# Four edits to an encoder kernel: GpSimd's order in the scan, VectorE's order beside the convolution taps, the place of the key sums, and the input norm's root

## The chip, the cores and the metric

The kernel runs on one core of a Trainium2 chip, in one launch. The metric is the device time of one execution in microseconds, the median of several. The engines of the core are TensorE (PE, matmuls and transposes; PEld are its weight loads), VectorE (DVE), ScalarE (ACT), GpSimd (POOL) and SyncE (SP), which here does nothing but issue transfers and wait. Each engine runs its own instructions in order; semaphores join them.

## The reference

A hybrid encoder layer is applied to two groups of tokens, 512 and 1024 of them, with model width 1024, in float32:

```
h = rms_norm(x);  p = h @ w_in                       # 4832 columns
z = centred_shift(p[RWKV columns]);  u = p[conv columns];  gates = sigmoid(rest)
A = rwkv7(z)      # 8 heads of 64, forward and reverse scans summed, group norm, bonus
B = silu(layer_norm(depthwise_conv31(glu(u))))
x = x + (gate_a * A @ W_o_rwkv + gate_b * B @ W_o_conv) @ w_out
x = x + expert_choice_ffn(rms_norm(x))               # 16 experts, each takes its top tokens
y = rms_norm(x)
```

with `rms_norm(x) = x * rsqrt(mean(x*x) + 1e-6) * g`. In the RWKV branch each direction has `decay = exp(-exp(logw))`, the keys are normalised per head (`kk / max(norm(kk), 1e-12)`), and per token and head the state follows `S = S diag(decay) + (S a) b^T + v k^T`, `y = S r`, with `a = -kk` and `b = kk * rate`.

## The kernel before

The kernel has five phases, one after the other: `project`, `scan`, `mixing`, `experts`, `final_norm`. The change touches the first two.

**project.** The 1536 tokens are three blocks of 512. The input is normalised first: ScalarE squares x, TensorE sums the squares into a PSUM bank with a matrix of ones, ScalarE takes the root (`root`, L618), VectorE the reciprocal (L811) and then scales x by it (L802); ScalarE splits the result into a high part, VectorE and GpSimd take the low part. Then 38 tiles of 128 columns are projected. Each product is made of three matmuls (high x high, low x high, high x low), for eight slices k of the contraction and three blocks: 72 matmuls of 128x512 per tile. From tile 2 on, small units of TensorE's work are put between the slices of a tile, at the places that `small_units` gives as (tile, k). They share two PSUM banks in turn, so unit u waits until unit u - 2 has been read (`emptied`).

The tiles stand in the order `ORDER`: two low-rank tiles, then four groups of eight (key, value, receptance, conv gate, conv input, three merge gates), then the remaining merge gates. Engines other than TensorE go through steps s = 1 to 38; step s treats tile s - 1 while TensorE works on tile s. Each group has six pieces (three blocks in two directions), one per step, from the group's fourth step on. For a piece p:

- TensorE makes two "rate" products at k = 1 and 2; ScalarE turns them into f0 and f1 by a sigmoid (`rates`, L695), after it has copied the next tile's weights (`high`, L607).
- VectorE scans f0 into f2 (`decay_sum`, L889), GpSimd takes the difference (L571), ScalarE three exponentials (L701, L703, L705), GpSimd writes AR (L579, L584).
- VectorE does `factors` (L898 to L910): it needs f1 and the first exponential f3 and writes KB.
- In the next step TensorE transposes both in three units "turn" at k = 4, 5, 6, ScalarE copies them out (L729), SyncE stores them.

Between `decay_sum` and `factors` VectorE has its share of the convolution: 31 taps per group, three to six in a step (`taps_at`, L846; the last, tap 30, is L850 and writes `conv`, which SyncE stores). In the step after the second tile of a group the keys are normalised: three "keys" units (L498), `key_max` (L876), logarithm and exponential on ScalarE (L744, L748), `key_normalise` (L882), and three "values" transposes.

SyncE's order in one step is: the load of the next weight tile (L347); the store of the first turned copy; a wait for GpSimd's last product and the store of AR (L404); the other stores of the last piece (L361, L369); a wait for VectorE's KB and its store (L414); in the step of tap 30 a wait for it and the conv store (L419).

**scan.** The recurrence is done in 24 chunks of 64 tokens, both directions side by side. Chunk i has a chain step `body(i)` on TensorE, which starts with `level_n(d, i, 0)` (L1175) and needs X0, the chunk's inverted 16x16 blocks placed on a diagonal. These are prepared ahead: masked products of chunk i + 4 are made in chain step i, stored (`lower`) and loaded again as 16x16 blocks of a pair of chunks (`diagonal`, gb); GpSimd inverts the pair (`invert`, L1399 to L1406: one addition, 14 rounds of two small instructions, a copy); SyncE stores the result (`inverses`, L1096) and loads it per chunk (`compact`, L1107, xc); GpSimd places it (`expand`, L1414, once for each direction). `expand` waits for xc and for the chain step two back. GpSimd's loop has, for even i, the inversion of pair i/2 + 1 and then the placement for chunk i + 1; for odd i the placement alone.

Of the kernel before, what the change touches and what calls it, by code (L numbers as in the profile page):

```python
# [9 lines left out]
ACT = mybir.ActivationFunctionType  # L10
# [4 lines left out]
D = 1024  # L15
# [190 lines left out]
def small_units():  # L206

    units = {}
    for s in range(N_TILES):
        p, last = piece_at(s), piece_at(s - 1)  # L210
        if p is not None:
            units[s, 1], units[s, 2] = ("rate", p, 0), ("rate", p, 1)
        if last is not None:
            for n in range(3):
                units[s, 4 + n] = ("turn", last, n)
            if last % 2 == 1:
                units[s, 7] = ("bonus", last // 2, 0)
        if s - 2 in GROUP_AT:
            hp = GROUP_AT.index(s - 2)
            for b in range(NB):  # L220
                units[s, b], units[s, 4 + b] = ("keys", hp, b), ("values", hp, b)
    return units


# [11 lines left out]
def project(nc, a, g):  # L236


    with ExitStack() as ctx:
        sb = lambda name, shape, dt=F32: ctx.enter_context(nc.sbuf_tensor(name, shape, dt))  # L240
        sem = nc.alloc_semaphore
# [35 lines left out]
        square = [halves(2 * (NB if b != 1 else 2)) for b in range(NB)]  # L277

        x_in = [[sem(f"p_x_in{b}{h}") for h in range(2)] for b in range(NB)]
        squared, halved, summed, rooted, normed = (  # L280
            sem(f"p_{n}") for n in ("squared", "halved", "summed", "rooted", "normed"))
        up_split, dup_in, rank_high, rank_low = (sem(f"p_{n}") for n in ("up_split", "dup_in", "rank_high", "rank_low"))
        h_high_done, h_low_v, h_low_p = sem("p_h_high_done"), sem("p_h_low_v"), sem("p_h_low_p")
        up_in, w_in, w_high_done, w_split = sem("p_up_in"), sem("p_w_in"), sem("p_w_high_done"), sem("p_w_split")
# [56 lines left out]
        with nc.Block() as block:  # L341
# [260 lines left out]
            def _(act):  # L602
# [12 lines left out]
                def root(b):  # L615
                    act.wait_ge(summed, 2 * b + 2)
                    act.wait_ge(normed, KD * b)
                    nc.scalar.activation(inv, g.bank[6 + b % 2][:], ACT.Sqrt, bias=g.c("eps", 0, 1),  # L618
                                         scale=1.0 / D).then_inc(rooted, 1)

                def h_top(b):
                    for n in range(4):
# [161 lines left out]
            def _(dve):  # L784
# [23 lines left out]
                ch.link(ts(mu_own[:], mu_own[:], -1.0, 1.0, ALU.mult, ALU.add))  # L808
                for b in range(NB):
                    dve.wait_ge(rooted, b + 1)  # L810
                    ch.link(nc.vector.reciprocal(inv, inv))  # L811
                    if b == 1:
                        fold(2)
                    scale(b, range(0, 4))
                    low(b, 0)
                    scale(b, range(4, KD))
                    low(b, 3)
# [74 lines left out]
                def factors(p):  # L892
                    hp, b, d = piece(p)
                    dve.wait_ge(a_rate, 2 * p + 2)
                    own_k = f4 if d else k_first
                    if d:
                        dve.wait_ge(m_bonus, p // 2)
                    ch.link(ts(own_k, f1, -1.0, g.v("k_a", hp), ALU.add, ALU.mult))  # L898
                    ch.count(stt(own_k, own_k, 1.0, key[:, tok(b)], ALU.add, ALU.mult))
                    dve.wait_ge(v_nkk, NB * (hp + 1))  # L900
                    ch.link(stt(f1, f1, -1.0, nkk[:, tok(b)], ALU.mult, ALU.mult))
                    dve.wait_ge(a_exp, 3 * p + 1)
                    dve.wait_ge(kb_out, 16 * p)
                    dve.wait_ge(m_turn, 3 * p)
                    tt(KB[:, :, 0, :], four(own_k), four(f3), ALU.mult).then_inc(v_k, 1)
                    tt(KB[:, :, 1, :], four(f1), four(f3), ALU.mult).then_inc(v_b, 1)
                    dve.wait_ge(v_k, p + 1)
                    if d:
                        ch.link(tt(f4, f4, k_first, ALU.add))
                        stt(f4, f4, g.v("r_k", hp), val[:, tok(b)], ALU.mult, ALU.mult).then_inc(v_w, 1)  # L910

                for s in range(1, N_TILES + 1):
                    t, tile = s - 1, ORDER[s - 1]
                    if tile < N_CONV and tile % 2 == 0:
                        convolve_in(t, tile // 2)
                    elif tile >= T_LORA:
                        shift(t, tile)
                    if s == 3:
                        rank_rest()
                    if s - 1 in GROUP_AT:  # L920
                        key_scale(GROUP_AT.index(s - 1))
                    if s - 2 in GROUP_AT:
                        key_max(GROUP_AT.index(s - 2))
                    p, taps = piece_at(s), taps_at(s)
                    if p is not None:
                        decay_sum(p)
                    for i, tap in taps:
                        convolve(i, tap)
                    if s - 2 in GROUP_AT:
                        key_normalise(GROUP_AT.index(s - 2))  # L930
                    if p is not None:
                        factors(p)


BASE = 16
# [4 lines left out]
def scan(nc, a, g):  # L940


    DIRS = range(2)
# [4 lines left out]
    with ExitStack() as ctx:  # L948
# [78 lines left out]
        with nc.Block() as block:  # L1027
# [358 lines left out]
            def _(pool):  # L1386
# [35 lines left out]
                for d in DIRS:  # L1422
                    expand(d, 1)
                for i in range(1, NCH - 1):
                    if i % 2 == 0 and i + 2 < NCH:
                        invert((i + 2) // 2)
                    for d in DIRS:
                        expand(d, i + 1)

            @block.vector  # L1430
            def _(dve):
# [1408 lines left out]
```

## Time and profile before

| | |
|---|---|
| median of 3 runs | 2781.54 us (2779.42 to 2785.18) |
| the profiled execution | 2781.26 us |
| its span, first to last instruction | 2779.5 us |
| TensorE busy | 2469.4 us (89%) |
| VectorE busy | 1842.3 us (66%) |
| ScalarE busy | 1200.2 us (43%) |
| GpSimd busy | 745.6 us (27%) |

`project` runs to about 837 us of the span, `scan` from there to about 1310 us. Times in the rows below are counted from the start of the span. In a row of the timeline the number in brackets is how long the engine sat idle before the instruction, with what ended that; "x4" means four like instructions merged into one row, and the duration is then from the first start to the last end. SPq and ACTq are transfers being issued; the duration is that of the issue, not of the transfer. The granted clock is 1.00 where TensorE runs at its full 2.4 GHz and 0.50 where it runs at 1.2 GHz. Names like `work` are one large buffer with many parts.

### The profile page before, as it was taken

Reading aid. Unit: us, or ns where it says so; the run is one execution under the profiler, and the core shown is the slowest. Engines: PE = TensorE matmul, PEld = TensorE weight load, DVE = VectorE, ACT = ScalarE, POOL = GpSimd, SP = SyncE. Lnnn points to the kernel's source line nnn. Section 1 sums busy time; section 2 is a strip of 40 time slices with the busy share of each in tenths; the row PEclk is TensorE's granted clock in tenths of the full one; section 3 lists DMA queues with packets and bytes.
Section 4 is the critical chain, followed back from the end, with each engine's and each line's share of the span. In section 5 each row is a group of like instructions: output and inputs, shape, how many; then the busy total and the mean of one; then the engine's idle time right before and its main releaser. Section 6 shows DMA issues by size and latency. Waiting matters only on the chain. (4 is left out here: it accounts for less than half of the span.)

```text
span 2779.5 us, 50229 instructions
## 1 busy us (share of the span) xinstructions
PE 2469.4 (89%) x19612; PEld 2083.9 (75%) x19612; DVE 1842.3 (66%) x2471; ACT 1200.2 (43%) x1746; POOL 745.6 (27%) x689
## 2 busy tenths in 40 slices
PE   6999989999895799897499899499999999999992
PEld 4777767777675788887267676399889998899991
DVE  7448868678674455554585857577777777777773
ACT  4443444334421233332233431365555656555552
POOL 3134342443420334332444533200101110001100
PEclk9999999999996899999699999699999999999996
DMA  3234243342435566652454543677777777777745
GB/s 129 73 106 129 72 138 98 117 130 80 134 127 160 153 173 178 170 141 77 150 191 164 192 155 114 256 231 247 239 255 237 228 247 241 245 247 229 246 162 200
DMA packets 294149, 476.87 MB, mean 172 GB/s; under 512 B 142048, under 2 KB 209776, under 8 KB 266336
## 3 DMA queue, kind: packets, MB, share of 16 engines
q1 hardware_dynamic: 280048, 428.25, 47.3%
q0 software_dynamic: 7680, 26.82, 4.7%
q10 hardware_dynamic: 6256, 19.47, 2.0%
q8 instruction: 120, 1.97, 0.3%
q14 instruction: 45, 0.37, 0.0%
HBM read 362.20 MB, written 110.69 MB: 170 GB/s over the span
## 5 line engine op out<-in xcount | busy, mean ns | idle before, releaser
L2499 PE MATMUL bank<-e_xt,e_w_high 128*128 128x384 f32 x1792 | 525.4, 357 | 1.3 <-DVE e_xt L2635 1.3
L2622 DVE TENSOR_TENSOR e_w_low<-e_w,e_w_high 128x2048 fp32r<-128x2048 f32 x192 | 436.2, 2286 | 95.8 <-ACT e_w_high L2555 95.8
L2500 PE MATMUL bank<-e_xt,e_w_low 128*128 128x192 f32 x1792 | 449.4, 251 | 0.0
L2555 ACT ACTIVATE e_w_high<-e_w 128x2048 fp32r<-128x2048 f32 x192 | 366.1, 1908 | 108.5 <-PE bank L2521 82.3
L2500 PEld LDWEIGHTS bank<-e_xt,e_w_low 128*128 128x128 f32 x1792 | 342.6, 191 | 0.6
L2499 PEld LDWEIGHTS bank<-e_xt,e_w_high 128*128 128x128 f32 x1792 | 338.4, 189 | 2.7 <-issue 1.4
L846 DVE SCALAR_TENSOR_TENSOR work<-work,vec 128x1551 f32<-128x1551 f32 x116 | 278.6, 2402 | 3.2
L463 PE MATMUL bank<-h_high,w_high 128*128 128x512 f32 x864 | 267.9, 419 | 0.3 <-DVE work L863 0.3
L466 PE MATMUL bank<-h_low,w_high 128*128 128x512 f32 x864 | 250.0, 398 | 0.0
L469 PE MATMUL bank<-h_high,w_low 128*128 128x512 f32 x864 | 247.5, 395 | 0.0
L2445 POOL DMA_INDIRECT xacc_dram<-e_y,e_put x32 | 50.3, 1573 | 731.6 <-DVE e_y L2657 726.8
L560 POOL TENSOR_TENSOR w_low<-w,w_high 128x1024 fp32r<-128x1024 f32 x38 | 94.0, 2475 | 436.7 <-ACT w_high L607 436.7
L466 PEld LDWEIGHTS bank<-h_low,w_high 128*128 128x128 f32 x864 | 165.9, 192 | 37.2
L469 PEld LDWEIGHTS bank<-h_high,w_low 128*128 128x128 f32 x864 | 165.6, 192 | 36.7
L463 PEld LDWEIGHTS bank<-h_high,w_high 128*128 128x128 f32 x864 | 154.3, 192 | 46.7 <-issue 24.0
L2666 DVE TENSOR_TENSOR e_sums<-bank,e_sums 128x192 f32<-128x192 f32 x256 | 79.3, 351 | 140.6 <-ACT e_sums L2580 140.6
L1748 POOL TENSOR_TENSOR x_w_low<-x_w,x_w_high 128x1024 fp32r<-128x1024 f32 x48 | 119.4, 2488 | 178.3 <-ACT x_w_high L1994 178.2
L889 DVE TENSOR_TENSOR_SCAN work<-con,work 128x512 f32<-128x512 f32 x24 | 57.0, 2375 | 152.2 <-issue 88.4
L2580 ACT ACTIVATE e_sums<-bank 128x192 f32<-128x192 f32 x256 | 70.6, 328 | 153.6 <-PE bank L2503 153.5
L607 ACT ACTIVATE w_high<-w 128x1024 fp32r<-128x1024 f32 x38 | 40.2, 1057 | 212.9 <-DMA w<-in_w_in 212.9
L1325 ACT ACTIVATE xx<-bank 128x512 f32<-128x512 f32 (+1 forms) x96 | 47.1, 491 | 158.7 <-PE bank L1188 97.4
L2459 PE MATMUL bank<-e_w_high,e_hid_parts 128*128 128x512 f32 x256 | 104.7, 409 | 0.0
(313 smaller groups left out, 5313.2 us busy)
## 6 DMA issues: line engine op xcount, KB each, us to landing
e_w<-in_ew SPq DMA_DIRECT2D x192, 1024.0 KB, 5.5
features_dram<-work SPq DMA_DIRECT2D x48, 512.0 KB, 3.2
fe<-features_dram SPq DMA_DIRECT2D x24, 1024.0 KB, 6.5
x_w<-in_w_mix SPq DMA_DIRECT2D x48, 512.0 KB, 3.8
w<-in_w_in SPq DMA_DIRECT2D x38, 512.0 KB, 4.6
ba_tok_dram<-work SPq DMA_DIRECT2D x96, 128.0 KB, 2.3
gates_dram<-work ACTq DMA_DIRECT2D x16, 768.0 KB, 4.1
all<-ba_tok_dram SPq DMA_DIRECT2D x96, 128.0 KB, 3.1
```

The costliest lines, as they stand in the source:

```text
L463: nc.tensor.matmul(bank(t, b)[:], w_high[t % 2][:, c], h_high[:, k, tok(b)], start=(k == 0), stop=False)
L466: nc.tensor.matmul(bank(t, b)[:], w_high[t % 2][:, c], h_low[:, k, tok(b)], start=False, stop=False)
L469: mm = nc.tensor.matmul(bank(t, b)[:], w_low[t % 2][:, c], h_high[:, k, tok(b)], start=False, stop=(k == KD - 1))
L560: tt(w_low[t % 2][:], w[:], w_high[t % 2][:].bitcast(F32), ALU.subtract).then_inc(w_split, 1)
L846: ch.link(stt(acc, cin[:, tap:tap + n_acc], wt, acc, ALU.mult, ALU.add))
L1748: tt(w_low[s % 2][:], w[s % 2][:], w_high[s % 2][:].bitcast(F32), ALU.subtract).then_inc(w_split, 1)
L2459: nc.tensor.matmul(out, left[0], right[0], start=first, stop=False)
L2499: nc.tensor.matmul(*wide, start=(k == 0), stop=False)
L2500: nc.tensor.matmul(*narrow, start=False, stop=False)
L2555: nc.scalar.activation(w_high[n % RING][:], w[n % RING][:], ACT.Copy).then_inc(w_high_done, 1)
L2622: tt(w_low[n % RING][:], w[n % RING][:], w_high[n % RING][:].bitcast(F32), ALU.subtract)\
L2666: ins = tt(half, g.bank[4 + 2 * (f % 2) + side][:, 0:SLOTS], half, ALU.add)
```

## The change

1. `small_units`: the key units of a group's second tile go from k = 0, 1, 2 to k = 1, 2, 4, the value units from 4, 5, 6 to 5, 6, 7.
2. `root`: instead of a square root on ScalarE and a reciprocal on VectorE, ScalarE takes the logarithm of the mean square and the exponential of minus one half of it.
3. VectorE in `project`: of a step's taps only the first stays ahead of `key_normalise` and `factors`; the others follow them.
4. GpSimd in `scan`: in an even step the placement for chunk i + 1 comes first, the inversion second.

```diff
-                units[s, b], units[s, 4 + b] = ("keys", hp, b), ("values", hp, b)
+                units[s, (1, 2, 4)[b]], units[s, 5 + b] = ("keys", hp, b), ("values", hp, b)
...
-                    nc.scalar.activation(inv, g.bank[6 + b % 2][:], ACT.Sqrt, bias=g.c("eps", 0, 1),
-                                         scale=1.0 / D).then_inc(rooted, 1)
+                    nc.scalar.activation(inv, g.bank[6 + b % 2][:], ACT.Ln, bias=g.c("eps", 0, 1),
+                                         scale=1.0 / D).then_inc(logged, 1)
+                    act.wait_ge(logged, b + 1)
+                    nc.scalar.activation(inv, inv, ACT.Exp, scale=-0.5).then_inc(rooted, 1)
...
-                    ch.link(nc.vector.reciprocal(inv, inv))
...
-                    for i, tap in taps:
+                    for i, tap in taps[:1]:
                         convolve(i, tap)
                     if s - 2 in GROUP_AT:
                         key_normalise(GROUP_AT.index(s - 2))
                     if p is not None:
                         factors(p)
+                    for i, tap in taps[1:]:
+                        convolve(i, tap)
...
                 for i in range(1, NCH - 1):
+                    for d in DIRS:
+                        expand(d, i + 1)
                     if i % 2 == 0 and i + 2 < NCH:
                         invert((i + 2) // 2)
-                    for d in DIRS:
-                        expand(d, i + 1)
```

## Rows read from the trace of the kernel before

**Rows 1.** Waits of TensorE, 100 to 830 us: total, times, longest in us.

```profile
PE bank L493 <- ACT work L695: 30.9, 12, 4.8
PE bank L498 <- DVE work L876: 6.5, 3, 2.7
```

**Rows 2.** The same view, 912 to 1310 us.

```profile
PE bank L1175 <- POOL x L1414: 38.3, 15, 10.2
```

**Rows 3.** Timeline of GpSimd in `scan`: start, duration, then the instruction.

```profile
1010.11 0.73 POOL L1399 TENSOR_TENSOR xb<-gb,masks 128x256 f32<-128x256 f32 x1 [10.50 <-DMA gb<-g_dram]
...
1021.46 2.04 POOL L1414 TENSOR_TENSOR x<-xc,masks 128x512 f32<-128x512 f32 x2
1034.30 2.04 POOL L1414 TENSOR_TENSOR x<-xc,masks 128x512 f32<-128x512 f32 x2 [10.80 <-DMA xc<-x_dram]
```

**Rows 4.** Timeline of SyncE, the same stretch.

```profile
1008.22 0.99 SPq L1107 DMA_DIRECT2D xc<-x_dram  x2
...
1027.04 0.49 SPq L1096 DMA_DIRECT2D x_dram<-xb  x1
...
1031.62 1.10 SPq L1107 DMA_DIRECT2D xc<-x_dram  x2
```

**Rows 5.** Timeline of TensorE, starts of two odd chain steps.

```profile
952.94 1.37 PE L1175 MATMUL bank<-x,nl 64*64 64x64 f32 x18 [10.19 <-POOL x L1414]
...
1022.55 0.68 PE L1175 MATMUL bank<-x,nl 64*64 64x64 f32 x16 [2.80 <-POOL x L1414]
```

**Rows 6.** Windows of odd chain steps: length, busy per engine, clock, DMA share, GB/s.

```profile
1022.50:1039.40 16.90, 16.53 (x384) 15.78 (x384) 8.85 (x17) 5.41 (x11) 3.03 (x3) 0.90 0.51 127
1056.60:1072.10 15.50, 15.18 (x386) 14.40 (x386) 8.92 (x17) 5.41 (x11) 3.47 (x3) 1.00 0.51 128
...
1123.10:1140.80 17.70, 17.70 (x384) 17.04 (x384) 8.84 (x17) 5.41 (x11) 2.95 (x3) 0.84 0.41 107
1159.70:1176.30 16.60, 16.55 (x384) 15.84 (x384) 8.88 (x17) 5.41 (x11) 3.03 (x3) 0.90 0.45 110
```

**Rows 7.** Timeline of GpSimd, another even placement.

```profile
1172.34 2.04 POOL L1414 TENSOR_TENSOR x<-xc,masks 128x512 f32<-128x512 f32 x2 [11.64 <-DMA xc<-x_dram]
```

**Rows 8.** Windows of two tiles with key sums.

```profile
277.30:302.30 25.00, 22.45 (x92) 16.99 (x92) 20.97 (x18) 12.15 (x17) 2.81 (x1) 0.93 0.20 57
...
113.30:133.70 20.40, 20.40 (x92) 15.83 (x90) 7.76 (x10) 11.36 (x16) 2.39 (x1) 1.00 0.11 31
```

**Rows 9.** Timelines of VectorE and SyncE in one step of `project`.

```profile
404.11 10.31 DVE L846 SCALAR_TENSOR_TENSOR work<-work,vec 128x1551 f32<-128x1551 f32 x4
...
412.82 0.36 SPq L404 DMA_DIRECT2D features_dram<-work  x1
...
415.53 1.25 SPq L369 DMA_DIRECT2D k_tok_dram<-work  x1
417.63 0.39 SPq L414 DMA_DIRECT2D features_dram<-work  x1
```

**Rows 10.** Waits of SyncE, 100 to 830 us.

```profile
SPq L414 <- DVE work L906: 40.1, 22, 4.4
```

**Rows 11.** Timelines of VectorE and SyncE in a step with tap 30.

```profile
340.57 3.01 DVE L850 SCALAR_TENSOR_TENSOR work<-work,vec 128x512 f32<-128x512 f32 x2
...
346.80 0.36 SPq L414 DMA_DIRECT2D features_dram<-work  x1
```

**Rows 12.** Timelines of ScalarE and VectorE in the input norm.

```profile
16.84 1.28 ACT L618 ACT_TABLE_LOAD   x1
...
54.08 0.67 ACT L618 ACTIVATE work<-bank,con 128x512 f32<-128x512 f32 x1
...
55.41 3.34 DVE L811 RECIPROCAL work<-work 128x512 f32<-128x512 f32 x1
```

**Rows 13.** Timeline of ScalarE behind the logarithm of the keys.

```profile
465.12 1.28 ACT L748 ACT_TABLE_LOAD   x1
466.42 1.68 ACT L748 ACTIVATE work<-work 128x512 f32<-128x512 f32 x3
```

More of the change, by code:

```diff
@@ L279, in project @@
         x_in = [[sem(f"p_x_in{b}{h}") for h in range(2)] for b in range(NB)]
-        squared, halved, summed, rooted, normed = (
-            sem(f"p_{n}") for n in ("squared", "halved", "summed", "rooted", "normed"))
+        squared, halved, summed, logged, rooted, normed = (
+            sem(f"p_{n}") for n in ("squared", "halved", "summed", "logged", "rooted", "normed"))
         up_split, dup_in, rank_high, rank_low = (sem(f"p_{n}") for n in ("up_split", "dup_in", "rank_high", "rank_low"))
```

## Prediction

> **What bounds the kernel.** The change touches the first two phases, `project` and `scan`, so I read them alone: first the waits of TensorE, then the engines behind each wait in order of time, then windows for the clock. In both phases TensorE is the pacemaker, and its waits are few and named. In `project` [rows 1] it waits 30.9 us, 12 times, for ScalarE's sigmoids at L695 (in front of a transpose, because the PSUM bank has to be free) and 6.5 us, three times, for VectorE's L876 (in front of the third key sum). In `scan` [rows 2] it waits 38.3 us for GpSimd's L1414, which places the inverted 16x16 blocks. Each class belongs to one of the edits. A reader should see next whether the awaited instruction is late through its own inputs or through its place in a queue, and what stands behind it when it is moved.
>
> **Edit 1, blocks ahead of the inversion (scan).** In every even step GpSimd inverts a pair of chunks and only then places the blocks of the next, odd chunk. [Rows 3]: the inversion starts at 1010.11, the two placements at 1021.46, so it takes 11.35 us, and TensorE starts that chain at 1022.55 after 2.80 us of idleness [rows 5]. The blocks were requested at 1008.22 and 1.0 later [rows 4]; a request of this kind lands 2.7 us after its issue (1031.62 in [rows 4], placement at 1034.30 in [rows 3]), so they lie there at about 1011.9, ten microseconds before they are used. Placed first, they are done at 1011.9 + 2.04 = 1013.9, and the wait goes; the largest, 10.19 us at 952.94 [rows 5], goes likewise. All 38.3 us hang on this one order.
>
> The stall also costs clock. The chain step after a short stall takes 15.5 us at granted clock 1.00 (full, the 2.4 GHz level); after stalls of 2.8 us and more they take 16.6 and 16.9 us at 0.90, 17.7 us at 0.84, so part of them ran at the 1.2 GHz level [rows 6]. Six steps follow such a stall and are as slow (the rows, 1.1 to 2.2 us too long, stand for them); six at 1.5 us give 9 us, and the step after the first stall I leave aside.
>
> What is moved back: the inversion starts at 1013.9 instead of 1010.11 and ends at 1025.2. Its result leaves only at 1027.04, since SyncE is still issuing other transfers [rows 4], so nothing is late by that; the blocks of the next even chunk are placed at 1034.30 to 1036.34 as before, and its chain started at 1039.4 [rows 3, 6], with 3.1 us to spare. The pair of steps, however, gets shorter by 2.8 + 1.4 = 4.2 us, so a wait of about 1 us appears there. Elsewhere the even blocks are placed later in the pair: 1172.34 to 1174.38 [rows 7], for a chain that starts at 1176.3 [rows 6], 1.9 us of slack against a saving of some 5: 3 us are late next. Over ten pairs, most with more slack than this last one, I take 5 us back (bounds 0 and 12). Sum: 38.3 + 9 - 5 = 42 us. Bounds: 38.3 - 12 = 26 (no clock back, all pairs tight) and 38.3 + 12 = 50.
>
> **Edit 2, key sums later (project).** The tile with the first key sums, at 113.3, has no wait and takes 20.4 us; the next of its kind takes 25.0 us at clock 0.93 [rows 8], because the third sum needs a bank that VectorE has not read yet. Moved from places 0, 1, 2 to 1, 2, 4, the third comes two products later (a place is some 2 us: the 20.4 us of the tile less the units' 4, over eight) plus the shifts, about 4 us, more than the longest wait (2.7 [rows 1]). This tile gives 4.6 us; the two others have the remaining 3.8 us of the 6.5 [rows 1] and little clock to regain, about 4.5: 9 us. The value transposes move one place back, so SyncE's last store of values and the weight load behind it, and with them the next sigmoids, are about 2 us later; they have room, as no transpose waits for a sigmoid in the next tile. Bounds: 5 (a remnant wait in each) and 10.
>
> **Edit 3, factors ahead of most taps (project).** The sigmoids wait for ScalarE's copy of the next weights, which waits for their transfer, which SyncE issues behind the store of KB, which waits for VectorE's factors; and these stood behind four taps, 10.31 us [rows 9]. It looks like 7.7 us per piece (three taps). But SyncE first waits for GpSimd's last factor and then issues the stores of the previous piece: 412.82 the AR store, 415.53 the k store, taking 1.25, and KB at 417.63 [rows 9]. KB could go at 416.8: 0.85 us earlier, not 7.7. GpSimd's chain (scan, difference, exponential, two products) does not depend on the taps. SyncE's 22 waits for KB sum to 40.1 us, at most 4.4 [rows 10], and the longest stand in the first step of a group, where the next transpose has time to spare. So three of the six pieces of a group give 0.3 to 2.2 us each, some 3 us per group, carried along from one late step to the next.
> In the step with tap 30 it is different: SyncE also waits there for the last tap, since the conv store stands between KB and the weight load. Now the last tap, L850, ends at 343.58, the factors follow, and KB goes at 346.80 [rows 11]: factors 3.2 us. Behind them come the two instructions of the bonus, about 1.4 at 0.7 each. In the new order these 4.6 us lie ahead of L850, which would end at 343.58 + 4.6 = 348.2. Its scan starts some 3 us sooner (the first step's long KB wait is gone), but the factors then wait 1 to 2 us for their exponential: about 346.4. Then conv store and load go, 0.4 us sooner than today, and KB's issue of 0.4 is already past: 0.8 gained. The longest waits of the phase, 4.8 us [rows 1], stand in the tiles after these steps, and stay, with the clock they cost.
> Sum: four groups of about 2.5 us with their share of clock: 8 us (I take off some, as the weight load then competes with stores issued just before it). Bounds: 0 (the landing does not move) and 16 (all gaps with their clock). VectorE's work in a step is 10.3 of taps, 3.2 to 4.6 of factors and some 3 of scan, 16.5 to 18 us where a tile takes 20 and more, so the taps are not late; its new wait for the exponential of the same piece costs 1 to 2 us of that idleness, with only taps queued behind it.
>
> **Edit 4, ln and exp for the root.** VectorE's reciprocal takes 3.34 us, ScalarE's root before it 0.67 [rows 12]. Instead ScalarE loads a table, 1.28, takes ln, loads again, 1.28 [rows 13], and takes exp; ln and exp I price as the root, for the same shape: 1.28 + 0.67 + 1.28 + 0.67 = 3.9 us against 0.67 + 3.34 = 4.0. Block 0: the first load stands there already [rows 12], so 1.28 + 0.67 replace 3.34: 1.4 us earlier. Block 1: nothing of its own, but it starts earlier by that gain, less a little for the later load of x. Block 2: from 54.08 the new chain ends at 58.0; the reciprocal, begun at 55.41, ended at 58.75: 0.7 more. TensorE waits for the normalised input in each block: 1.7 us. Bounds: -1 (the third x block, whose load now goes 2 us later, is late) and 2.5.
> The trace has ln and exp with a load each, and the first activation starts 0.02 us after a load [rows 13]. The Trainium skill ("ScalarE: Activation LUTs", sections "What ACT_TABLE_LOAD costs" and "Table sets: the hidden batching unit") says otherwise on both: a switch costs 1.28 us plus a drain of 1.38, and one set holds ln and exp. By its drain the new chain would be 2.8 us longer, and this edit would cost about 1 us instead of giving 1.7; by the shared set it would give 1.3 us more per block. The trace shows neither, and I go by it.
>
> **Sum.** 42 + 9 + 8 + 1.7 = 61 us. The profiled execution took 2781.26 us (its span 2779.5), 0.3 from the median of 2781.54, so 2781.3 - 61 = 2720 us. What comes after `scan` waits for its end and moves as a whole; the taps that run out after the last piece end with the same distance to TensorE's end as now.
>
> **Rivals.**
> A. *The freed time is taken back by the even chains* (SyncE and the transfers set the pace of a pair of steps): for it speaks that the even placements wait for the transfer of their blocks (10.80 and 11.64 us [rows 3, 7]) with 2 to 3 us to spare; against it, that GpSimd's inversion is not what SyncE waits for. Then only the slack and the first stall come: 10.19 and the slack, 9 x 1.9 = 17, so 27 with no clock, and with a tap gain of 2 the sum is 27 + 9 + 2 + 1.7 = 40: 2741.
> B. *The factors remove all the sigmoid waits*: the 30.9 us [rows 1] and, at 1.5 us for each of some ten tiles, 15 us of clock: 46 instead of 8. Time 2720 - 38 = 2682. For it speaks the chain as written in the code; against it [rows 9, 11].
> C. *Slower: the inversion slips behind the blocks.* If the odd blocks land L us after the inversion's input, the inversion ends L + 2.04 + 11.35 after it; its result leaves 16.9 after it now (1027.04 - 1010.11 [rows 3, 4]), and the even chain has 3.1 to spare. So from L = 6.6 each even chain is late by the rest, and the whole kernel is slower when ten pairs lose more than edits 2 to 4 give: 10 x (L - 6.6) > 19, L above 8.5. With L = 10, and the odd chains no better off than now: 2781 + 34 - 19 = 2796. Against it: L is 1.8 here.
> D. *The new order does nothing*, since the placement of the odd blocks waits for TensorE as well (two chains back): 2781 - 19 = 2762. Against it: where a placement waited, it waited for the transfer [rows 3, 7].
>
> **How the numbers follow.** Forecast 0.62 (2705 to 2735), A 0.22, B 0.07, D 0.04, C 0.05. The lower bounds of all edits together give 26 + 5 + 0 - 1 = 30 us, the upper ones 50 + 10 + 16 + 2.5 = 78: the range 2700 to 2750 takes these and A in and leaves B, C and D out. A change under 0.2% (5.6 us) can't be told from none here. Faster 0.94, same 0.02, slower 0.04.
>
> **What would show it.** In the profile after: TensorE's wait for L1414 (x) all but gone in odd steps and small in even ones, chain steps of 15 to 15.5 us at clock 1.00, `scan` about 42 us shorter; GpSimd's placements in pairs right before each inversion. In `project`: no wait in front of the key sums; the sigmoid wait still 4 to 5 us in the tile after tap 30, three times, and 1 to 4 in the two tiles of a group that had it. TensorE's first product at about 26.3 instead of 27.7. I am wrong if even chains wait over 1 us each in the mean (A), or if the sigmoid waits sum to under 10 us (B).

## The result, and the profile after

The changed kernel takes 2710.25 us in the median of 4 runs (2705.57 to 2715.02), the kernel before beside it 2780.48: a ratio of 0.9755, 95% interval 0.9716 to 0.9795. The forecast was 2720, range 2700 to 2750. The profiled execution of after took 2707.34 us, its span 2705.6, which is 73.9 less than before. By stages of the span: up to tile 2 it is 1.6 us shorter, tiles 2 to 37 34.3 us, from there to the first chain step 3.0, chain steps 0 to 23 36.8, and the rest is 1.9 longer.

Two windows carry most of it; the columns are as in [rows 6]. First before, tiles 2 to 37 and chain steps 0 to 23, then the same work after:

```profile
80.60:814.10 733.50, 695.93 (x3073) 542.77 (x3074) 520.50 (x383) 304.13 (x381) 263.25 (x131) 0.97 0.37 111
892.73:1293.53 400.80, 350.79 (x8416) 333.97 (x8416) 214.48 (x390) 130.16 (x259) 149.33 (x376) 0.92 0.58 156
```

```profile
78.90:778.10 699.20, 681.83 (x3072) 534.33 (x3073) 505.50 (x382) 301.70 (x380) 220.74 (x131) 0.99 0.39 117
853.76:1217.77 364.01, 340.36 (x8416) 323.98 (x8417) 212.27 (x390) 130.08 (x259) 151.88 (x376) 0.96 0.64 171
```

The same matmuls keep TensorE busy 14.1 and 10.4 us less, at a higher granted clock; the rest of the 34.3 and 36.8 us is idleness that went. In `project` something else shrank that no edit touches in number or shape: GpSimd's busy time, from 263 to 221 us over the same 131 instructions.

TensorE's waits after, in `project` (answers to [rows 1]; the wait for the key maxima is gone) and in `scan` (to [rows 2]; this window also holds 6.2 us in front of chain step 1, which lies ahead of the window of [rows 2] and was 5.8 there):

```profile
PE bank L493 <- ACT work L697: 17.3, 9, 3.7
```

```profile
PE bank L1178 <- POOL x L1417: 12.6, 5, 6.2
```

GpSimd in one pair of chain steps (answers to [rows 3]): the placement of the odd blocks stands right in front of the inversion, whose first instruction is L1402 and whose last is L1409; the even placement still waits for its transfer. (The profile names L1195 of TensorE as what ended the first wait; why it was a transfer there too is said under rival D.)

```profile
957.88 2.04 POOL L1417 TENSOR_TENSOR x<-xc,masks 128x512 f32<-128x512 f32 x2 [7.96 <-PE bank L1195]
959.88 0.73 POOL L1402 TENSOR_TENSOR xb<-gb,masks 128x256 f32<-128x256 f32 x1
...
970.63 1.05 POOL L1409 COPY xb<-xb 128x256 f32<-128x256 f32 x1
978.68 2.04 POOL L1417 TENSOR_TENSOR x<-xc,masks 128x512 f32<-128x512 f32 x2 [7.00 <-DMA xc<-x_dram]
```

Windows of chain steps 7, 8 and 13 (answers to [rows 6]) and of the tile with the second key sums (to [rows 8]):

```profile
271.00:291.40 20.40, 20.40 (x92) 15.84 (x92) 15.38 (x16) 11.33 (x16) 2.39 (x1) 1.00 0.14 44
968.98:983.93 14.95, 14.95 (x388) 14.30 (x385) 9.50 (x18) 6.00 (x12) 4.29 (x9) 1.00 0.56 139
983.93:1000.23 16.30, 15.22 (x388) 14.43 (x384) 10.05 (x19) 6.00 (x12) 9.03 (x24) 1.00 0.85 246
1060.22:1079.30 19.08, 16.70 (x389) 15.92 (x385) 9.72 (x19) 6.00 (x12) 7.21 (x19) 0.91 0.62 168
```

A step without idleness takes 14.95 us; nine of the 23 do, of either parity. The two longest take 19.1 and 19.2 us (13 and 17): TensorE stops inside each, the first time for 2.38 us, with nothing that the profile shows to wait for. The largest wait for a placement is in front of chain step 22. TensorE, two starts:

```profile
1065.72 0.37 PE L1195 MATMUL bank<-x,t 64*64 64x64 f32 x1 [2.38 <-issue]
```

```profile
1203.09 1.69 PE L1178 MATMUL bank<-x,nl 64*64 64x64 f32 x24 [3.84 <-POOL x L1417]
```

### The profile page after: what moved, and what is told of

The parts are those of the page before. It is cut to its first block and busy times, and to the rows that moved or that the text cites. A ratio compares the mean times of both kernels' runs of the same rounds, so it can differ in the third digit from the quotient of the medians.

```text
span 2705.6 us, 50239 instructions
## 1 busy us (share of the span) xinstructions
PE 2443.5 (90%) x19612; PEld 2062.2 (76%) x19612; DVE 1817.4 (67%) x2468; ACT 1205.4 (45%) x1753; POOL 704.2 (26%) x689
## 5 line engine op out<-in xcount | busy, mean ns | idle before, releaser
L2558 ACT ACTIVATE e_w_high<-e_w 128x2048 fp32r<-128x2048 f32 x192 | 365.9, 1908 | 108.6 <-PE bank L2524 82.4
L847 DVE SCALAR_TENSOR_TENSOR work<-work,vec 128x1551 f32<-128x1551 f32 x116 | 216.1, 1863 | 2.4
L560 POOL TENSOR_TENSOR w_low<-w,w_high 128x1024 fp32r<-128x1024 f32 x38 | 91.0, 2396 | 441.3 <-ACT w_high L607 441.3
L1417 POOL TENSOR_TENSOR x<-xc,masks 128x512 f32<-128x512 f32 x48 | 49.4, 1046 | 250.3 <-DMA xc<-x_dram 242.4
```

Of the source, the lines that this page charges most:

```text
L560: tt(w_low[t % 2][:], w[:], w_high[t % 2][:].bitcast(F32), ALU.subtract).then_inc(w_split, 1)
L847: ch.link(stt(acc, cin[:, tap:tap + n_acc], wt, acc, ALU.mult, ALU.add))
L2558: nc.scalar.activation(w_high[n % RING][:], w[n % RING][:], ACT.Copy).then_inc(w_high_done, 1)
```

## The experiments

Ten kernels ran, each timed beside the kernel before. In short (ratios with their 95% interval; "to chain 0" is where the first chain step starts in the span, 892.7 before and 853.8 after):

| kernel | edit | median, us | ratio | to chain 0 |
|---|---|---|---|---|
| e1_blocks | edit 1 alone | 2735.29 | 0.985 (0.9809 to 0.9892) | 886.4 |
| e2_taps | edit 3 alone | 2748.32 | 0.9901 (0.9872 to 0.993) | 858.5 |
| e3_keys | edit 2 alone | 2776.73 | 1.0007 (0.9985 to 1.0028) | 889.6 |
| e4_root | edit 4 alone | 2773.63 | 0.9991 (0.9974 to 1.0009) | 887.7 |
| e5_kb_late | before; weight load ahead of KB's store | 2752.69 | 0.9915 (0.9886 to 0.9945) | 858.7 |
| e8_ends_last | e5; copy of the ends behind the product | 2744.78 | 0.9887 (0.9856 to 0.9918) | 858.3 |
| e9_ends_act | e5; that copy on ScalarE | 2746.63 | 0.9899 (0.9883 to 0.9916) | 857.8 |
| e10_no_tap_ahead | after; no tap ahead of the factors | 2706.33 | 0.9754 (0.9738 to 0.977) | 851.6 |
| e6_load_early_old | before; weight load ahead of all waits | 2724.23 | 0.9803 (0.9772 to 0.9834) | 835.1 |
| e7_load_early_new | after; the same | 2680.47 | 0.9661 (0.9634 to 0.9689) | 828.3 |

The kernel before measured 2776.34 us beside e1 to e4, 2775.41 beside e5 to e8 and 2774.88 beside e9 and e10. The last column is from one profile each: e1, whose `project` is that of before, has 886.4 where before has 892.7, so differences of up to some 6 us say nothing there.

Where the time of tiles 2 to 37 goes is seen best by kinds of tile (sums in us, from the starts of the tiles in one profile each). The rows are the tiles behind tap 30 (15, 23, 31), two sets that also wait for sigmoids (9, 17, 25, 33 and 10, 18, 26, 34), the tiles whose key sums waited (12, 20, 28), and the rest. e4, which changes nothing in these tiles, shows how much one profile says: up to 7 us in a row, mostly moved from one row to the next, and 3 in the sum.

| tiles | before | e4 | e2 | e3 | e5 | after | e10 | e6 | e7 |
|---|---|---|---|---|---|---|---|---|---|
| 15, 23, 31 | 81.6 | 82.7 | 77.9 | 87.3 | 66.0 | 77.1 | 82.9 | 60.9 | 60.9 |
| 9, 17, 25, 33 | 100.8 | 94.0 | 82.4 | 97.4 | 94.3 | 83.1 | 81.5 | 81.2 | 81.2 |
| 10, 18, 26, 34 | 86.0 | 91.2 | 85.1 | 87.3 | 82.2 | 84.6 | 80.4 | 78.5 | 78.5 |
| 12, 20, 28 | 70.6 | 67.8 | 64.6 | 61.2 | 64.6 | 61.2 | 61.2 | 62.3 | 61.2 |
| the rest | 394.5 | 395.2 | 392.9 | 397.2 | 393.5 | 393.2 | 393.2 | 392.9 | 393.2 |
| all | 733.5 | 730.8 | 702.8 | 730.4 | 700.5 | 699.2 | 699.2 | 675.9 | 675.0 |

### The four edits alone

```diff
# e1_blocks
                 for i in range(1, NCH - 1):
+                    for d in DIRS:
+                        expand(d, i + 1)
                     if i % 2 == 0 and i + 2 < NCH:
                         invert((i + 2) // 2)
-                    for d in DIRS:
-                        expand(d, i + 1)
# e2_taps
-                    for i, tap in taps:
+                    for i, tap in taps[:1]:
                         convolve(i, tap)
...
+                    for i, tap in taps[1:]:
+                        convolve(i, tap)
# e3_keys
-                units[s, b], units[s, 4 + b] = ("keys", hp, b), ("values", hp, b)
+                units[s, (1, 2, 4)[b]], units[s, 5 + b] = ("keys", hp, b), ("values", hp, b)
# e4_root: the logarithm and exponential of the change, no reciprocal
```

> The kernel before with edit 1 alone (GpSimd places the blocks ahead of the inversion). The forecast's theory: TensorE's waits for the placement (38.3 us) leave all odd chain steps and the clock comes back; scan from the first to the last chain step, 400.8 us before, comes to about 363 as in the changed kernel, project stays as it was, time about 2742 (-38). Rival (the parts need each other, since the phases share nothing but their border): another figure than the changed kernel's scan. Rival A (even chains take it back): over 370 us.

> The kernel before with edit 3 alone (factors ahead of most taps). Theory of the forecast (only the wait for KB goes): 8 us less, GpSimd's instructions as long as before (product L579 1.98 us, copy L582 1.63 us). New theory from the two traces (VectorE's taps beside GpSimd's work slowed it, and GpSimd's last product releases the stores and the weight load): L579 1.43 us, L582 0.50 us in the mean, TensorE's waits for the sigmoids 31 to about 17 us, project 25 us shorter, time about 2755.

> The kernel before with edit 2 alone (key sums at places 1, 2, 4). Theory: the 6.5 us of waits in front of the third key sum go, the three tiles take 20.4 us each, 9.3 us less: 2771. Rival: without the other edits VectorE is later, so that part of the wait stays: 3 to 6 us less.

> The kernel before with edit 4 alone (ln and exp for the inverse root). Theory: TensorE's first tile behind the three blocks starts 1.7 us earlier (78.9 instead of 80.6), nothing else changes: 2779. By the drain of 1.38 us that the Trainium skill names beside each table load (ScalarE: Activation LUTs, What ACT_TABLE_LOAD costs) it would start about 1 us later than before.

Against the 2776.34 beside them: -41.1, -28.0, +0.4 and -2.7 us, together -71.4, where all four at once gave -70.2. So the edits add up, but not as forecast (42, 8, 9, 1.7).

e1: TensorE's wait for the placements, 870 to 1310 us, a window that again holds chain step 1 (6.1 us; the 6.4 is in front of chain step 22):

```profile
PE bank L1175 <- POOL x L1414: 15.7, 6, 6.4
```

Chain steps 0 to 23 take 362.9 us (400.8 before). The four profiles with the new order (e1, e7, e10 and after) have 362.9 to 364.5 us here, the others with the old one 394.0 to 405.3, so the order is the cause. The even chains take back 9.6 us of waiting in e1, 6.4 in the changed kernel.

e3: the key tiles take 20.4 us, as forecast, and the sigmoids take it away again. TensorE's waits in `project`:

```profile
PE bank L493 <- ACT work L695: 40.1, 13, 6.8
```

Against [rows 1] the wait for L695 rises from 30.9 to 40.1 us; the tiles behind tap 30 go from 27.2, 27.8 and 26.6 us to 28.7, 28.8 and 29.8. The reason is VectorE. Between 255 and 350 us it waited before for L677, 5.2 us, and has no such pause in e3, first row before, second e3:

```profile
DVE work L859 <- ACT work L677: 5.2, 2, 4.9
```

```profile
DVE work L859 <- ACT work L677: 0.3, 1, 0.3
```

TensorE's 4.6 us in the key tile bring tap 30 only 3.0 us forward (its start goes from 340.6 to 337.6), because VectorE is the one that is full up to there. Tiles 2 to 37 are 3.1 us shorter in all, no more than in e4, and the time is the same. The rival comes nearer than the theory, but even its 3 to 6 us are not there.

e4: the 1.7 us can't be read off the span. Tile 2 starts at 79.3 in e4 (forecast 78.9, before 80.6), but at 78.4 in e1, which has the old root: this start shifts between profiles by more than the edit gives. Under edit 4 below, the gain is counted from the second square instead.

e2: with the taps moved alone, both waits fall, and so does the key wait, whose tiles and units this kernel leaves where they were (6.5 to 2.2 us). Edit 3 alone makes the three key tiles 6.0 us shorter, of the 9.3 in the changed kernel. Its waits:

```profile
PE bank L493 <- ACT work L695: 16.8, 8, 3.5
...
PE bank L498 <- DVE work L876: 2.2, 3, 1.0
```

### Which link of the loop: e5, e8, e9, e10

From one piece to the next there is a loop: scan, GpSimd's chain, store of AR, other stores, (KB), issue of the weight load, its landing, weights copied, sigmoids, next scan. In the step of [rows 9] it takes 11.5 + 5.3 + 5.6 + 1.7 = 24.2 us (scan to the store of AR, that to the issue of the load, landing, to the next scan), where a tile without a stall takes 19.5 to 20.3. After the change the same step has 9.8 + 5.0 + 6.1 + 1.7 = 22.6.

```diff
# e5_kb_late (before, SyncE's order)
+                ahead = [s for s in range(1, N_TILES - 2) if piece_at(s) is not None and (not taps_at(s) or taps_at(s)[-1][1] < TAPS - 1)]
...
-                    if s + 1 < N_TILES:
+                    if s + 1 < N_TILES and s - 1 not in ahead:
                         load(s + 1)
...
+                    if s in ahead:
+                        load(s + 2)
                     if p is not None:
                         sp.wait_ge(v_b, p + 1)
# e8_ends_last (e5; SyncE's wait, GpSimd's chain)
-                        sp.wait_ge(l_r, p + 1)
+                        sp.wait_ge(l_ar, p + 1)
...
-                    nc.gpsimd.tensor_copy(g.ends[:, d, hp, 8 * b:8 * b + 8], ...)
-                    tt(AR[:, :, 1, :], four(val[:, tok(b)]), four(f2), ALU.mult).then_inc(l_r, 1)
+                    tt(AR[:, :, 1, :], four(val[:, tok(b)]), four(f2), ALU.mult).then_inc(l_ar, 1)
+                    nc.gpsimd.tensor_copy(g.ends[:, d, hp, 8 * b:8 * b + 8], ...).then_inc(l_r, 1)
# e9_ends_act (e5): that copy is an activation on ScalarE
# e10_no_tap_ahead (after)
-                    for i, tap in taps[:1]:
+                    for i, tap in taps[:0]:
...
-                    for i, tap in taps[1:]:
+                    for i, tap in taps[0:]:
```

> The kernel before, taps in their old order; SyncE issues the next weight load ahead of the store of KB (not in the steps with tap 30). So the load no longer waits for VectorE's factors, while the taps still run beside GpSimd's work. Theory (two causes: the KB wait some 8 us, the slowed GpSimd instructions the rest of the 30): 8 to 12 us less in project, L579 and L582 as long as before (1.98 and 1.63 us). Rival (the KB wait was all, and my 8 us were mis-summed): as much as edit 3 alone gave, 28 us.

e5 brings the first chain step to 858.7, as e2 does (858.5), with the taps where they were: the loop of the same step is 11.6 + 2.7 + 6.6 + 1.7 = 22.5 us. In time it is -22.7 us where e2 is -28.0, with intervals that overlap: the theory's 8 to 12 us were far too few, the rival's 28 is nearer. In e2 nothing waits for KB either and GpSimd's chain is 1.7 us shorter besides, but KB's issue stays ahead of the load, and the loop of that step is 9.8 + 5.0 + 6.1 + 1.7 = 22.6 us, the same.

That the two sums are alike is chance, though, for the table above has them in different tiles. e5 takes 15.6 of its 33.0 us out of the tiles behind tap 30: in the first step of a group (13, 21, 29) the load now follows the store of AR by 0.4 us instead of 5.2. e2 gains 3.7 us there, since its factors now lie ahead of tap 30, for which SyncE waits, and 18.4 of its 30.8 us in tiles 9, 17, 25 and 33, where e5 gains no more than e4 differs by (6.5 and 6.8). The two loops ahead of tile 17 are 3.6 us shorter in e2, 3.3 of it in GpSimd's chain (9.3 to 7.6 and 11.5 to 9.9 us). So the wait for KB and GpSimd's chain are two causes, and each shows in tiles of its own.

The chain on GpSimd, 100 to 790 us (the columns: busy time, mean ns of one, idle time before them): before, then after.

```profile
L571 POOL TENSOR_TENSOR work<-work 128x512 f32<-128x512 f32 x24 | 61.1, 2545 | 27.9 <-DVE work L889 27.9
L579 POOL TENSOR_TENSOR work<-work 128x512 f32<-128x512 f32 x24 | 47.5, 1981 | 25.0 <-ACT work L703 25.0
L582 POOL COPY ends<-work 128x8 f32<-128x8 f32 x24 | 39.1, 1628 | 0.0
```

```profile
L571 POOL TENSOR_TENSOR work<-work 128x512 f32<-128x512 f32 x24 | 61.3, 2555 | 27.9 <-DVE work L890 27.9
L579 POOL TENSOR_TENSOR work<-work 128x512 f32<-128x512 f32 x24 | 34.4, 1433 | 28.9 <-ACT work L705 28.9
...
L582 POOL COPY ends<-work 128x8 f32<-128x8 f32 x24 | 12.0, 501 | 0.0
```

A copy of 128x8 takes 1.63 us before and 0.50 after; of 128x512, before, three instructions of one shape take 2.5, 2.0 and (L584, in both kernels) 1.3. The taps, beside which they stand, change as well: before, then after.

```profile
L846 DVE SCALAR_TENSOR_TENSOR work<-work,vec 128x1551 f32<-128x1551 f32 x102 | 248.9, 2440 | 2.7
```

```profile
L847 DVE SCALAR_TENSOR_TENSOR work<-work,vec 128x1551 f32<-128x1551 f32 x116 | 216.1, 1863 | 2.4
```

e8 and e9 ask how: if the copy is slow by itself, moving it away frees its time.

> As e5_kb_late, and GpSimd's copy of the ends (L582, 1.63 us) goes behind its last product, which alone releases the store of AR. Theory: GpSimd's chain sets the load of the weights, so the 1.6 us come off each late step: 10 to 16 us beyond e5_kb_late. Rival (SyncE's issues and the landing set it): nothing beyond e5_kb_late.

> The kernel before, with the next weights' load issued ahead of the store of KB in every step but those of tap 30 (as in e5), and GpSimd's copy of the chunk ends (1.4 us a piece there) given to ScalarE, behind its exponentials of the next piece. Theory 1 (GpSimd's chain of a piece, through the AR store on SyncE, sets when the load is issued): scan to AR store falls from 11.5 to about 10 us, `project` gets 5 to 15 us shorter than in e5, 2738 to 2748 us. Rival (what is slowed beside the taps is whatever GpSimd instruction stands there, as in e8, so the chain loses little): scan to AR store at 11 or more and a time within 5 us of e5's 2752.7. A second rival: the copy on ScalarE pushes its sigmoids or copies of weights back, and it is slower than e5.

Neither does: scan to AR store stays at 11.4 us in both (11.5 in e5), and the times are 7.9 and 6.1 us under e5's median (each against its own "before": ratios 0.9887 and 0.9899 beside 0.9915, intervals that overlap). Tiles 2 to 37 take 700.2 and 698.9 us where e5 has 700.5. That e9's time lies in its theory's 2738 to 2748 is luck: the chain did not get shorter. The product that moved into the copy's place takes 2.5 us instead of 1.3. First e8, then e9:

```profile
L585 POOL TENSOR_TENSOR work<-work 128x512 f32<-128x512 f32 x24 | 60.0, 2499 | 0.0
...
L586 POOL COPY ends<-work 128x8 f32<-128x8 f32 x24 | 31.2, 1301 | 0.0
```

```profile
L584 POOL TENSOR_TENSOR work<-work 128x512 f32<-128x512 f32 x24 | 60.4, 2518 | 0.0
```

The timelines say why. In the step of [rows 9] GpSimd's chain is this, and the second of the four taps is the row behind it:

```profile
404.26 2.80 POOL L571 TENSOR_TENSOR work<-work 128x512 f32<-128x512 f32 x1 [1.16 <-DVE work L889]
407.81 2.04 POOL L579 TENSOR_TENSOR work<-work 128x512 f32<-128x512 f32 x1 [0.74 <-ACT work L703]
409.80 1.74 POOL L582 COPY ends<-work 128x8 f32<-128x8 f32 x1
411.50 1.29 POOL L584 TENSOR_TENSOR work<-work 128x512 f32<-128x512 f32 x1
```

```profile
405.95 2.75 DVE L846 SCALAR_TENSOR_TENSOR work<-work,vec 128x1551 f32<-128x1551 f32 x1
```

The first tap runs alone from 404.11 [rows 9] to 405.9, 1.8 us; L571 was issued at 404.26, ends at 407.06, and that is 405.9 and nearly a whole L571 of 1.29 us. The second tap is issued at 405.95 and ends at 408.70, 1.8 us behind 406.9. L579 ends 1.15 us behind that, the third tap 1.8 us behind about 409.7; the copy ends with the third tap, at 411.54; L584 starts before the fourth tap and takes its 1.29. So the two engines take turns, one whole instruction each: each start and end fits that to about 0.2 us. In e9 the last product is issued at 395.71 into the third tap (394.63 to 397.39) and ends at 398.54:

```profile
395.71 2.83 POOL L584 TENSOR_TENSOR work<-work 128x512 f32<-128x512 f32 x1
```

```profile
394.63 2.75 DVE L851 SCALAR_TENSOR_TENSOR work<-work,vec 128x1551 f32<-128x1551 f32 x1
```

Dropping the copy only let the product run into that tap. What helps is a short instruction of VectorE at that place. After the change factors of 0.69 us stand there, and now they are the ones that wait (0.69 to 1.8 us):

```profile
392.35 1.79 DVE L902 SCALAR_TENSOR_TENSOR work<-work 128x512 f32<-128x512 f32 x1
394.18 1.81 DVE L906 TENSOR_TENSOR work<-work 128x512 f32<-128x512 f32 x1
```

The Trainium skill ("SBUF — State Buffer", section "Who interferes with whom") has this as a rule: VectorE and GpSimd share a port pair, and it is an exclusive lock; a VectorE instruction with two SBUF inputs contends with a GpSimd instruction that reads SBUF. That whoever issues first gets the pair "for the whole instruction" it says of VectorE's two-port modes. The trace agrees, and has whole turns for these two-input instructions as well, in numbers above. It was the rule that spoke against the forecast's size for edit 3, and the prediction did not weigh it.

> The changed kernel with no tap at all ahead of the factors (one was left there). Theory 1 (a tap beside GpSimd's difference L571 slows it to 2.55 us): L571 falls towards 2.0, scan to AR store from 9.8 to about 9.2 us, and the time is 3 to 10 us under the changed kernel's 2710. Rival: the first tap only filled VectorE's wait for the exponential of the same piece; VectorE then stands idle, its taps end later, the conv store behind tap 30 and the load behind it are later by one tap's 1.9 us in the three tap-30 steps, and the time is the same or up to 6 us longer.

The first tap, too, is such a holder: without it L571 falls from 2.56 to 1.45 us, and scan to AR store from 9.8 to 9.05 us in the plain steps. But the time is unchanged, a ratio of 0.9754 against 0.9755. TensorE's waits in `project` there:

```profile
PE bank L493 <- ACT work L697: 16.9, 5, 5.4
```

Five instead of nine, but the three tiles behind tap 30 wait 5.3 to 5.4 us each instead of 3.5 to 3.7: tap 30 is later. By the table, what is lost behind tap 30 (5.8 us) is won in the two rows below it. Both theories had a half of it.

### The load taken out of the loop: e6 and e7

```diff
+                ahead = [s for s in range(1, N_TILES - 2) if piece_at(s) is not None]
...
                     if last is not None:
                         staged(("turn", last, 0))
+                    if s in ahead:
+                        load(s + 2)
                     if p is not None:
                         hp, b, d = piece(p)
                         sp.wait_ge(l_r, p + 1)
```

> The kernel before, taps in their old order; in steps with a piece SyncE issues the next weight load right behind the first turned copy's store, ahead of its waits for GpSimd and VectorE. Theory (the weight load is the only way by which taps and factors reach TensorE): all sigmoid waits go, also those behind tap 30; project 45 us shorter, about 2732. Rival (ScalarE's sigmoid needs f1, that is VectorE's factors, in time): waits of 1 to 3 us stay in the steps with four taps.

> The changed kernel with the same early weight load. Theory: the 17.3 us of sigmoid waits and their clock, 25 us, leave project: about 2686, the fastest of all; its project is equal to that of e6_load_early_old but for the key sums (9 us), since the order of the taps then no longer matters. Rival (transfers compete: the load meets the stores of gates and turned copies): 10 us only.

In both TensorE waits for no sigmoid and no key maximum at all between 90 and 740 us, and the first chain step starts 51 to 58 us earlier in e6 and 58 to 64 in e7, by which of the two profiles of the old `project` one takes. So the load is the only way by which taps, factors and GpSimd's chain reach TensorE, and the rival of e6 falls; the granted clock is 1.00 over tiles 2 to 37 in both. In time e6 is -51.2 us, and e7, which has edit 1 as well, -94.9. e7 is the fastest kernel of the study: 2680.47 us, 24.7 us further below the kernel before beside it than the changed kernel is (-94.9 against -70.2), 29.8 by the bare medians. Its tiles 2 to 37 take 675.0 us where e6 has 675.9. With the load early neither the order of the taps nor the place of the key sums is worth anything there: the 9 us expected for the key sums are 1.1 in the three key tiles. Its SyncE in the same step: the load goes ahead of the store of AR, and its landing takes 3.8 us.

```profile
381.22 0.50 SPq L347 DMA_DIRECT2D w<-in_w_in  x1
385.19 0.36 SPq L407 DMA_DIRECT2D features_dram<-work  x1
```

## Why the prediction came out as it did

The sign and the time were right, and the mechanism of edit 1, which is the larger part. Of edits 2 and 3 the forecast had the waits right and the sizes wrong, one too large and one far too small; that their errors partly cancel is luck.

**Edit 1 (42): right.** -41.1 us alone. In the profiles chain steps 0 to 23 are 36.8 us shorter, 37.9 in e1. The waits fell from 38.3 to 6.4 (12.6 less the 6.2 of chain step 1), TensorE is busy 10.4 us less (the clock, forecast 9), and the even chains take 6.4 us of waiting (forecast 5). Its places were less good: chain step 8, for which 1 us was forecast, has none, chain step 16 0.8 instead of 3; the largest, 3.8, is at 22. The stops inside steps 13 and 17, 2.4 us each, were not foreseen.

**Edit 2 (9): too large.** In the changed kernel the three key tiles are 4.6, 1.6 and 3.1 us shorter, 9.3 in all, but 6.0 of that is there with edit 3 alone (e2), so beside edit 3 the edit is worth some 3 us; alone it gives nothing (e3). The step that failed is "they have room, as no transpose waits for a sigmoid in the next tile": the taps lie between, and VectorE, full up to tap 30, does not follow. "VectorE's work in a step is 16.5 to 18 us where a tile takes 20 and more, so the taps are not late" is the same error: in the key tile of [rows 8], 277.3 to 302.3, VectorE is busy 20.97 us, more than the 20.4 that the tile was to take.

**Edit 3 (8): the term that was most mis-sized, about 30 instead.** Tiles 2 to 37 lost 34.3 us; alone the edit gave 30.8 us there and 28.0 in time. The forecast let the load move by 0.85 us in three pieces of six. Two steps failed. One is "GpSimd's chain (scan, difference, exponential, two products) does not depend on the taps": it does, since it takes turns with them, and moving three of them away made it 1.7 us shorter. SyncE in the step after (answers to [rows 9]):

```profile
395.46 0.36 SPq L404 DMA_DIRECT2D features_dram<-work  x1
395.87 1.60 SPq L361 DMA_DIRECT2D ba_tok_dram<-work  x2
397.51 1.52 SPq L369 DMA_DIRECT2D k_tok_dram<-work  x1
399.08 1.36 SPq L414 DMA_DIRECT2D features_dram<-work  x1
400.49 1.02 SPq L347 DMA_DIRECT2D w<-in_w_in  x1
```

KB is hardly waited for any more (SyncE's 40.1 us of [rows 10] are 2.3), the loop is 1.5 us shorter, and the stalls that went gave clock back: TensorE is busy 14.1 us less in tiles 2 to 37. The other step that failed is "the longest stand in the first step of a group, where the next transpose has time to spare". The forecast took the gap between 416.8 and 417.6 for the whole cost of KB and set those first steps aside; e5, which changes this link alone, gives 22.7 us in time, and nearly half of what it takes off the tiles comes from them, one step on, in the tiles behind tap 30. No run shortens GpSimd's chain with nothing else changed, so how edit 3's 28 us divide between KB and the chain is read from the loops, not measured. The 3.0 us less from tile 37 to the first chain step mean nothing: that stretch takes 78.6 us in the profile of before and 75.2 in e1's, which has the same work there. Of the tap-30 step the forecast nearly held: its tiles wait 3.5, 3.7 and 3.5 us, from 4.8, 4.8 and 4.6, 1.1 to 1.3 less where 0.8 was forecast. What SyncE now waits for there is tap 30 itself, 14.8 us in these three steps (the fourth wait, 25.8, is behind the last piece), where before it never did:

```profile
SPq L419 <- DVE work L851: 40.6, 4, 25.8
```

**Edit 4 (1.7): right in size, too small to see.** Counted from the second square of the input the first product comes 0.6 us sooner (27.18 in the span, not 26.3), the third block 1.3 us; the time of e4 has an interval of both signs. ScalarE and the low part of h:

```profile
16.93 1.28 ACT L618 ACT_TABLE_LOAD   x1
18.22 0.69 ACT L618 ACTIVATE work<-bank,con 128x512 f32<-128x512 f32 x1
18.93 1.28 ACT L621 ACT_TABLE_LOAD   x1
20.22 0.63 ACT L621 ACTIVATE work<-work 128x512 f32<-128x512 f32 x1
```

```profile
24.58 2.54 DVE L799 TENSOR_TENSOR h_low<-work,h_high 128x1024 fp32r<-128x1024 f32 x1 [0.88 <-ACT h_high L627]
```

The chain on ScalarE is as priced, 1.28 + 0.69 + 1.28 + 0.63. The activation follows a load by 0.01 us, and logarithm and exponential take a load each: neither the drain nor the shared set of the Trainium skill that the prediction weighed shows here. What is missing at the first product is a turn again: VectorE's L799, issued at 24.58 while GpSimd works at L560 (23.68 to 26.05), takes 2.54 us where it took 1.21 before, when it was issued at 26.45.

**The rivals.** A (2741) fell: even chains wait 6.4 us in all, 0.6 a pair (9.6 and 0.9 in e1). B (2682) fell for this change, the sigmoids still wait 17.3 us; e6 shows that its price was about right (51.2 us in time, where B had 46 for the sigmoids and 9 for the keys) and that another edit was needed for it. D's mechanism is not there. The row says that the placement at 957.88 waited for TensorE (L1195, of chain step 6), but it needs only the one of chain step 5, which ended at 942.9. What it waited for is its blocks, requested at 955.53, with 2.3 us or more from issue to landing for these requests:

```profile
955.53 0.99 SPq L1110 DMA_DIRECT2D xc<-x_dram  x2
```

L1195 only happened to end at the same time, and the placement is done 9 us ahead of the chain step that needs it. C's mechanism is there: the inversion behind it ends at 971.68, its result is requested at 971.89, and the even placement ends at 980.72, 3.2 us ahead of its chain step at 983.93. In front of chain step 22 it costs something: the inversion, begun behind the placement at 1183.44, ended at 1195.23, its blocks were requested at 1198.40, the placement came at 1202.00, and TensorE waited 3.8 us.

**The sum.** 61 us was forecast, 70 measured. The 42 of edit 1 are 36.8 in the profile, the 17 of edits 2 and 3 are half of the 34.3 of tiles 2 to 37; with 2.8 elsewhere that is 73.9 us between the two spans. The medians of the two kernels are 70.2 apart, and 2710 lies in the range because the 42 outweigh the rest.

## What to carry to other kernels

Where an in-order queue issues both stores that wait for engines and the load that the next step needs, follow the whole loop from one load to the next, not the last wait in front of it: here one load moved ahead in SyncE's order is worth 51.2 us by itself (e6) and about 25 on top of the change (e7), and it makes edits 2 and 3 superfluous. Before an instruction is called independent of those beside it, look at its shape's durations elsewhere in the trace: a 128x8 copy of 1.6 us, or three equal products of 2.5, 2.0 and 1.3 us, were the sign here that VectorE and GpSimd take turns, and then long instructions of VectorE belong where GpSimd has no chain to run. A gain in front of an engine that is full is taken back by it (e3): test edits alone and together. And when two edits give the same time, compare them tile by tile before taking them for one cause (e2 and e5).

## What the runs showed of the hardware

- VectorE's two-input instructions and GpSimd's take turns by whole instructions: a tap of 1.8 us takes 2.75 when it is issued while GpSimd has its turn, a product of 1.29 us takes 2.8 when it is issued into a tap, and taking an instruction away from such a chain (e9) left its end where it was, at 11.4 us. One with a single input does so too: the 128x512 of L899 takes 1.40 us at 390.30 in the changed kernel, beside GpSimd's L571, and 0.49 us at 414.46 before (there L898), with no GpSimd instruction beside it.
- A stall costs clock as well, as in [rows 6]: in the two windows 46.6 us of TensorE's idleness went, and 24.5 us of its busy time with it, for the same matmuls. The 9 us of clock that the forecast counted in `scan` were 10.4; in `project` it counted only a few, and there were 14.1.
- From issue to landing the weight load takes 3.9 us in the mean where only the first turned copy's store is issued right ahead of it (e7, the steps with a piece from step 13 on), and in the same steps 5.4 before and 6.0 after, right behind the later stores of the turned copies and KB. That these transfers slow it was not tried by itself.
- Open: the two stops of 2.4 us inside chain steps 13 and 17, for which the profile names no cause. e1 and e7 have steps longer than 14.95 us there too (15.4 to 17.4), but not as long.
